# Routing the first tile of a product-key expert layer in two parts: eight experts first, the other eight after

## What is computed

```
q = (xt @ w_query).reshape(T, 8, 2, 128)
s = einsum('thpd,pkd->thpk', q, sub_keys)            # 128 scores for each of two halves
s_a, i_a = top_k(s[:, :, 0], 16)
s_b, i_b = top_k(s[:, :, 1], 16)
cand_s = (s_a[..., :, None] + s_b[..., None, :])     # 16 x 16 = 256 sums of a pair
cand_i = (i_a[..., :, None] * 128 + i_b[..., None, :])
top_s, pos = top_k(cand_s, 16)
idx = take_along_axis(cand_i, pos)                   # 16 experts of 16384
gate = softmax(top_s)
act = gelu(einsum('thkd,td->thk', u_tab[idx], x))
out = einsum('thk,thkd->td', gate * act, v_tab[idx])
```

## Times and profile before

| | |
|---|---|
| three runs, median | 2287.83 us (2286.14 to 2288.05) |
| the profiled execution | 2289.55 us |
| its span, first to last instruction | 2287.8 us |
| busy: PE, DVE, ACT, POOL | 1935.8, 1470.6, 669.0, 614.3 us |
| moved by the 512 gathers | 536.90 MB of 712.93 MB |
| mean granted clock of PE | 0.954 |

### The profile page before, as it was taken

One profiled execution on the slowest core, in us unless ns is written; L12 is line 12 of the kernel. 1 busy time (PEld: TensorE's weight loads), 2 busy tenths in 40 slices (PEclk: granted clock), 3 DMA queues, 4 the chain that ended last, 5 costly groups with the idle time before them and its releaser, 6 DMA issues.

```text
span 2287.8 us, 22080 instructions
## 1 busy us (share of the span) xinstructions
PE 1935.8 (85%) x6404; PEld 1125.8 (49%) x6404; DVE 1470.6 (64%) x3982; ACT 669.0 (29%) x1857; POOL 614.3 (27%) x588
## 2 busy tenths in 40 slices
PE   4999999868887887797779999998678888887876
PEld 3677777443443443343347777765333433433432
DVE  5476776766676666767525676666566676676765
ACT  1222322123333333333212222230233333333332
POOL 3000000034444344343300000000443434444442
PEclk9999999979999999999889999998899999999989
DMA  9354455269999999999943345431999999999995
GB/s 378 126 216 163 172 212 215 91 252 422 421 421 421 421 421 421 421 420 420 407 168 139 138 181 202 181 118 67 384 421 421 421 421 421 421 421 417 421 414 245
DMA packets 116332, 712.93 MB, mean 312 GB/s; under 512 B 12816, under 2 KB 17168, under 8 KB 48656
## 3 DMA queue, kind: packets, MB, share of 16 engines
q0 software_dynamic: 73728, 536.90, 56.6%
q1 hardware_dynamic: 42512, 174.97, 19.9%
HBM read 710.78 MB, written 1.05 MB: 311 GB/s over the span
## 4 chain that ended last, share of the span: by engine, by line
PE 44%; DMA 28%; DVE 17%; issue 4%; POOL 3%; ACT 2%; SPq 1%; DVEq 0%; POOLq 0%; ACTq 0%
DMA wall<-in_peer_uv,idx 26%; PE PS L869 12%; PE PS L691 9%; PE PS L696 7%; DVE wall L911 5%; PE PS L701 4%; PE PS L848 4%; POOL wall L485 3%; PE PS L677 2%; PE PS L761 1%; PE PS L707 1%; DVE braw L911 1%; ACT M L628 1%; DVE pos L1249 1%; DMA psc<-in_pool_scale 1%
## 5 line engine op out<-in xcount | busy, mean ns | idle before, releaser
L869 PE MATMUL PS<-wall,M 128*128 128x512 f32 x2048 | 981.4, 630 | 271.9 <-ACT M L628 270.9
L911 DVE CUSTOM_DVE_ANT_0 wall<-wall,tok 128x1024 f32<-128x1024 f32 x512 | 604.4, 1222 | 425.9 <-DMA wall<-in_peer_uv,idx 420.9
L869 PEld LDWEIGHTS PS<-wall,M 128*128 128x128 f32 x2048 | 396.9, 201 | 828.6 <-issue 434.7
L485 POOL DMA_INDIRECT wall<-in_peer_uv,idx x512 | 569.9, 1113 | 752.4 <-PE PS L869 354.1
L614 ACT ACTIVATE dg<-dg 128x2 f32<-128x2 f32 x256 | 52.1, 203 | 851.2 <-DVE dg L911 851.2
L691 PE MATMUL PS<-hT,wall 128*128 128x256 f32 x1120 | 247.9, 380 | 0.2 <-DMA wall<-in_w_in 0.2
L447 POOL TENSOR_SCALAR rsb<-ms 128x4 f32<-128x4 f32 (+2 forms) x23 | 5.4, 236 | 890.1 <-DVE ms L911 890.0
L691 PEld LDWEIGHTS PS<-hT,wall 128*128 128x128 f32 x1120 | 211.6, 190 | 30.4 <-issue 0.6
L696 PE MATMUL PS<-wall,hT 128*128 128x512 f32 x512 | 224.7, 592 | 0.0
L628 ACT ACTIVATE M<-ident,wgt 128x128 f32<-128x128 f32 x512 | 177.5, 394 | 24.6 <-ACT wgt L621 1.1
L696 PEld LDWEIGHTS PS<-wall,hT 128*128 128x128 f32 x512 | 96.2, 190 | 108.9 <-issue 108.1
(11 more groups left out here) (211 smaller groups left out, 1696.9 us busy)
## 6 DMA issues: line engine op xcount, KB each, us to landing
wall<-in_w_in SPq DMA_DIRECT2D x128, 704.0 KB, 11.0
braw<-in_ada_rows SPq DMA_DIRECT2D x80, 512.0 KB, 4.7
ring<-in_peer_w_query SPq DMA_DIRECT2D x14, 1024.0 KB
wall<-in_w_out SPq DMA_DIRECT2D x2, 4096.0 KB, 16.9
wall<-in_peer_uv,idx POOLq DMA_INDIRECT x512
wall<-in_ada_rows SPq DMA_DIRECT2D x6, 1024.0 KB, 12.4
pwt<-in_pool_w SPq DMA_DIRECT2D x8, 256.0 KB, 5.0
wall<-in_peer_w_query SPq DMA_DIRECT2D x2, 1024.0 KB, 4.8
```

The costliest lines, as they stand in the source:

```text
L485: nc.gpsimd.indirect_dma_start(out=pair_rows[b][s], out_offset=None, in_=uv_rows, in_offset=bass.IndirectOffsetOnAxis(ap=idx[t][:, k:k + 1 ...
L869: i = mm(bank(B_ACC + 2 * t + hf), diag[:, b, s, :], pair_rows[b][s][:, D + hf * 512:D + (hf + 1) * 512], start=False, stop=(g // HGROUPS ...
L911: return v.tensor_tensor_reduce(out=o, in0=a, in1=b, scale=1.0, scalar=0.0, op0=ALU.mult, op1=ALU.add, accum_out=acc)
```

## The change

Only the first tile of each layer is concerned (head 0, tile 0). Its routing on DVE is written in a new order. `best_first` takes the eight highest of each half with their positions, forms the 8 x 8 sums, takes the eight highest of those with one MAX and one MAX_INDEX, and turns the positions into expert numbers as `route_pairs` does, with shift 3 and mask 7 in place of 4 and 15 and with arrays of 2 x 8 x 8 in place of 2 x 16 x 16. It writes columns 0 to 7 of `idx[0]` and signals a new semaphore, `s_best`. After that it strikes the eight out of each half, takes the next eight, and the unchanged `route_pairs` runs over all 256 sums; `route_end` then writes columns 8 to 15 alone. The eight highest of all 256 sums have ranks in both halves of at most eight, so both ways name the same experts.

POOL waits for `s_best` before the first gather of a layer, and for `s_route` before the ninth (group 4). No gather is added or taken away, and PE and ACT have the same lists as before.

```diff
+EARLY = 8
...
-                    if q == 0:
+                    if g == 0:
+                        pool.wait_ge(s_best, l + 1)
+                    elif q == 0 or g == EARLY // GROUP:
                         pool.wait_ge(s_route, 2 * HEADS * l + h * NT + t + 1)
...
+                def best_first():
+
+                    dve.wait_ge(s_psc0, l + 1)
+                    halves = [bank(B_SC)[:, a * P:(a + 1) * P] for a in range(2)]
+                    few = slice(0, EARLY)
+                    apart(dve)
+                    for a in range(2):
+                        ch(v.max(out=sv[:, a, few], in_=halves[a]))
+                    ch.sync()
+                    apart(dve)
+                    for a in range(2):
+                        ch(v.max_index(iu[:, a, few], sv[:, a, few], halves[a]))
+                    sums = cand[:, 0:EARLY * EARLY]
+                    ch(v.tensor_tensor(sums.rearrange("p (a b) -> p a b", a=EARLY),
+                                       sv[:, 0, few].unsqueeze(2).to_broadcast([P, EARLY, EARLY]),
+                                       sv[:, 1, few].unsqueeze(1).to_broadcast([P, EARLY, EARLY]), ALU.add))
+                    ch.sync()
+                    apart(dve)
+                    ch(v.max(out=ts[:, few], in_=sums))
+                    ch(copy(idf[:, :, few], iu[:, :, few]))
+                    ch.sync()
+                    apart(dve)
+                    ch(v.max_index(pos[:, few], ts[:, few], sums))
+                    ch.sync()
+                    ch(sts(ab[:, 0, few], pos[:, few], 3, None, ALU.logical_shift_right, ALU.bypass))
+                    ch(sts(ab[:, 1, few], pos[:, few], 7, None, ALU.bitwise_and, ALU.bypass))
+                    ch.sync()
+                    ch(copy(abf[:, :, few], ab[:, :, few]))
+                    ch.sync()
+                    square = [P, 2, EARLY, EARLY]
+                    hit = oneh[:, :, few, few]
+                    ch(v.tensor_tensor(hit, abf[:, :, few].unsqueeze(3).to_broadcast(square),
+                                       iota16[:, few].unsqueeze(1).unsqueeze(1).to_broadcast(square), ALU.is_equal))
+                    ch.sync()
+                    ch(v.tensor_tensor(hit, hit, idf[:, :, few].unsqueeze(2).to_broadcast(square), ALU.mult))
+                    ch.sync()
+                    ch(v.tensor_reduce(red[:, :, few], hit, AX, ALU.add))
+                    ch.sync()
+                    ch(stt(idfl[:, few], red[:, 0, few], float(P), red[:, 1, few], ALU.mult, ALU.add))
+                    ch.sync()
+                    sts(idx[0][:, few], idfl[:, few], float(NEXP * l), None, ALU.add, ALU.bypass).then_inc(s_best, 1)
+                    for a in range(2):
+                        ch.sync()
+                        ch(v.match_replace(out=wk, in_to_replace=sv[:, a, few], in_values=halves[a], imm_value=-3.4e38))
+                        ch.sync()
+                        top8(sv[:, a, EARLY:TOPK], iu[:, a, EARLY:TOPK], wk)
...
-                    sts(idx[t][:], idfl[:], float(NEXP * l), None, ALU.add, ALU.bypass).then_inc(s_route, 1)
+                    k = slice(EARLY if first else 0, TOPK)
+                    sts(idx[t][:, k], idfl[:, k], float(NEXP * l), None, ALU.add, ALU.bypass).then_inc(s_route, 1)
...
-                route_half(0, 0, 0, True)
-                route_half(0, 0, 1, True)
+                best_first()
                 route_pairs(0, 0)
```

More of the change, by code:

```diff
@@ L283, in build @@
         s_gate, s_wgt = sem("s_gate"), sem("s_wgt")
+        s_best = sem("s_best")
         s_peer = sem("s_peer")
@@ L1268, in route_half @@
+                def route_half(h, t, a):
+                    if a == 0:
                         dve.wait_ge(s_psc, h + (HEADS * l + 1))
```

## The result

| | median | range | ratio to before, 95% interval |
|---|---|---|---|
| before | 2287.94 us | 2286.14 to 2290.63 | |
| changed | 2275.15 us | 2272.32 to 2277.34 | 0.9939, 0.9926 to 0.9951 |

The changed kernel is 12.8 us faster (forecast: 11.9 us, 2275.9). Its profiled execution took 2274.41 us with a span of 2272.3 us. Later runs of both kernels gave 0.9941 (0.9928 to 0.9955) and 0.9948 (0.9934 to 0.9962); 11.9 us is 0.9948.

A forecast was written before the change was run, and what follows sets the result against it. The prediction took a stream of 256 gathers, late to start because of DVE's routing, to bound the expert part. Starting it 5.95 us earlier in each of two layers gave 11.9 us, 2287.83 to 2275.9 us, range 2273.5 to 2280.8.

The forecast's parts named there:

- The bound: Expert part of each layer: a stream of 256 gathers at 421 GB/s, some 640 us, nothing else scarce; its start counts.
- (a): DVE path from first MAX8 to first indices: 3.89 us instead of 9.84, so 5.95 us earlier in each layer.
- (b): Rest of the routing on DVE, behind the first indices: DVE done 2.75 us later, hidden while group 0's data arrive.
- the cover: Group 0 lands at 481.4, 1.3 us after DVE is free, which hides DVE's later finish of the routing.
- (c): POOL's added wait for `s_route` ahead of the ninth gather: no wait at all.
- The margin of 11 us: How late `s_route` could come before the eight early gathers run out: some 11 us.
- (e): Gathers 2 to 8 on POOL beside `route_pairs`: a step of at most 2.29 us, under 2.49; cost taken as zero.
- The sum: Whole kernel: the stream moves as a whole, 2 x 5.95 = 11.9 us, median from 2287.83 to 2275.9 us.
- (1): Rival, 0.09: stretched first gather, dear small products and DVE's late finish leave 4.0 us a layer, 8 us, 2280.
- (2): Rival, 0.06: gain lost again in a gap at the ninth gather or a later buffer wait; 2287 to 2288 us.
- (3): Rival, 0.02: something else holds the first gather; routing longer by 2.75 us lands on both layers' path; 2293 us.
- (4): Rival, 0.02: DVE blocks POOL's gathers 2 to 8; decides above 3.2 us a step; at 4 us, 2300.

The follow-up runs named there:

- without early gathers: Changed kernel, but POOL waits for `s_route` also before the first gather of each layer: 2294.04 us, ratio to before 1.0021.
- the delay ahead: Changed kernel with six idle DVE products, 4.45 us, before the first MAX8 of each layer's first tile: 2288.01 us, in a second session 2286.95 us.
- the best expert alone: Changed kernel, but column 0 of the indices is written right after the two MAX_INDEX and gather 0 starts on it: 2271.34 us, ratio to before 0.992.
- eleven idle products: Changed kernel with eleven unused DVE products, 8.0 us, between `best_first` and `route_pairs` in each layer: 2275.34 us, ratio to before 0.995.
- changed, again: Unchanged copy of the changed kernel, run for a second profile: 2274.96 us, ratio to before 0.9941.

## Why the prediction was right

**The bound.** It said that the expert part is a stream of 256 gathers that is moved as a whole. From the first gather to the last dot product layer 1 took 663.86 to 664.28 us in the five profiles of the two kernels, and delays ahead of it counted while one of 8 us behind its start did not. Over all kernels whose stream did not pause, this holds within two microseconds (662.98 without early gathers, 666.03 with the delay ahead). One reading was too simple: "some 640 us" and "nothing else in it is scarce". 256 gathers at 2.49 us make 637 us, and layer 1 needs 664, layer 0 673. The same 421 GB/s also carry weights: in layer 0 of the kernel before, the queue of SyncE issues six transfers of 1 MB of `w_query` between 515 and 930 us, and from 1123.77 those of the next mixer, and there the last two groups come 8.46 us apart in place of 4.98. Both kernels issue the same transfers, so the forecast did not depend on it.

**(a) The path.** 3.89 us were summed and 3.85 and 3.86 measured. The steps that no row had: the product on 64 elements took 0.20 us (0.22 taken), MAX8 on 64 elements 0.23 (0.23), the products on 2 x 8 x 8 and the reduction 0.29 each (0.29 and 0.28). The upper bound, that small views don't get cheaper, was far off.

**(b) The rest of the routing.** 8.69 us were forecast between the two writes of indices (470.89 to 479.58), 9.08 measured. Of the missing 0.4 us, 0.35 are the wait shown above ahead of MATCH_VALUE_LOAD, 0.46 us where a gap of 0.11 is usual behind MAX8. The gathers aren't its cause. The kernel without early gathers has the same wait at the same instruction, 6.4 us after the first MAX8, and its first gather starts 7.6 us later, at 482.10:

```profile
474.46 0.09 DVE L1254 MATCH_VALUE_LOAD iu<-sv,M 128x8 f32 x1 [0.46 <-DVE sv L1251]
```

With operations put in ahead of it (the delay ahead of the first MAX8, the best expert alone) the wait stands at an earlier instruction. What it is stays open.

Group 0 landed 9.4 us after the first gather started in both kernels, and DVE still waited 0.93 us for it (1.3 forecast). With the cover gone, in the kernel with eleven idle products and in the one with the best expert alone, no price could be seen in the medians, as stated.

**(c) The added wait** was none: 0.30 us ahead of the ninth gather. The margin of 11 us is bracketed by the delays of 8 us (free) and 16 us (5.4 us of pause worked out, 4.8 us in the first three windows).

**(e) Gathers beside routing.** Of gathers 2 to 8 of layer 0, six took 0.94 us and one 1.30. The prediction had only a bound for this, 1.99 us. The rows tell what lengthens a gather: an operation of DVE with two inputs in on-chip memory (a product or a dot product) that is under way when the gather starts.

| profile, gather of layer 0 | operation of DVE under way | left of it at the gather's start | the gather took |
|---|---|---|---|
| changed, 5th (477.62) | none with two inputs; a product starts at 477.94 | 0 | 0.94 |
| delay ahead, first profile, 9th (489.04) | dot product from 487.96 | 0.15 | 0.96 |
| changed, again, 9th (481.46) | dot product from 480.45 | 0.22 | 1.03 |
| before, 9th (488.18) | dot product from 487.38 | 0.43 | 1.23 |
| changed, 6th (478.86) | one-hot product from 478.66 | 0.49 | 1.30 |
| no early gathers, 9th (492.32) | dot product from 491.76 | 0.67 | 1.48 |
| changed, 9th (482.96) | dot product from 482.91 | 1.17 | 1.98 |

Each gather took 0.94 us plus what was left of the operation, less 0.13; a product that starts after the gather does not lengthen it. The same sum gives 6042 of the 6144 gathers in the twelve profiles within 0.06 us. Most of the others are first gathers of a layer (1.07 to 1.22 us), gathers beside the idle products (whose rows are merged), and gathers that started at most 0.03 us behind the start of a dot product and still took 0.94. The Trainium skill (SBUF — State Buffer, "Who interferes with whom") says that a DVE instruction with two inputs in SBUF contends with a GpSimd instruction that reads SBUF, and that the shared ports are an exclusive lock, which the one that comes first keeps for its whole instruction. The rows agree, up to the last 0.13 us. The other direction shows in the kernel with the best expert alone: a CAST of DVE took 0.39 us in place of 0.18 and ended with gather 6 (477.44). Beside the idle products gathers took about 1.15 us:

```profile
480.82 1.15 POOL L490 DMA_INDIRECT wall<-in_peer_uv,idx  x1 [0.31 <-issue]
482.28 1.14 POOL L490 DMA_INDIRECT wall<-in_peer_uv,idx  x1 [0.30 <-issue]
```

There a gather starts every 1.45 us, which is two products of 0.73 us, so each of them meets a product at the same point. The longest gather behind the first of a layer took 2.00 us in all twelve profiles, a step of 2.3 us with the 0.30 behind it, still under the 2.49 us that its data take. So the bound of the prediction, 1.99 us, was right.

**The sum.** 11.97 us by the paths in the traces, 12.8, 14.4 and 12.1 us by the medians of three sessions, 11.9 forecast and inside all three intervals. The median was 0.75 us under the forecast. The forecast allowed 1.7 us for the spread of the runs. The traces show where a spread of this size comes from: the start of the first routing lies anywhere from 465.89 to 468.09 in the five profiles, and mixer 1 between 438.37 and 442.14. That the median came within 0.75 us of the forecast is in part luck.

**The rivals.** (1), part of the gain: each of its three losses was near zero. (2), a gap at the ninth gather: shown only when 16 us were put in. (3), a longer routing that lands on the path: the kernel without early gathers is that case, and costs 4.7 us, where 5.5 were worked out. (4), starved transfers: the longest step of POOL before the ninth gather was 1.6 us in layer 0 (1.30 and 0.30) and 1.7 us in layer 1 (1.43 and 0.30), and the longest in any kernel with the change 2.2 us (1.89 and 0.30, in the one with the change in layer 0 alone), under 3.2.

## What to carry to other kernels

Where a stage is a stream of transfers at its full rate, as here at 421 GB/s, expect the serial work ahead of its first transfer to count one to one, and work behind the first transfers to count next to nothing until the queue is empty. So split whatever makes the indices or addresses: find the smallest part of them that can be had early, start with it, and let each further part arrive before the last one has been moved (here one index covered 2.5 us, eight covered 20). A small first piece can make the total work longer, here by 3 us a layer, and still win. Without the early start the same order loses (4.7 us here).

## What the runs showed of the hardware that was not expected

The same eight products took 3.7 us in one profiled execution of a program and 6.7 us in another, at granted clocks of 1.00 and 0.55. Among the last groups of layer 0 in the twelve profiles (all that have a row of their own behind 1090 us), those with at most 1.8 us of idle time of PE in front always took 3.70 us, and those with 3.6 to 4.8 us always 5.1 to 6.8 us. In between, at 2.1 to 3.3 us, it went either way: 3.70 us in eleven cases, 5.1 to 5.4 us in five, 6.7 us in two. A slow group leaves a shorter idle stretch ahead of the next, which often was a fast one, but not always: in the third profile of the changed kernel three in a row took 5.40, 5.12 and 5.40 us. Which kind falls last is not the same in every execution. At the end of layer 0 it stands on the path, so that two single profiles of equal kernels can differ by 3 us there; a difference of one pair of profiles has to be cut into stretches before it is believed.

A gather of POOL that starts while DVE is in an operation with two inputs in on-chip memory lasts longer by what is left of that operation, less 0.13 us (0.94 us alone, 1.98 us when it starts 0.05 us behind a dot product).
